# Layer 1's attention in groups of four heads: one PSUM bank per unit, plain transpositions, normalisation at the output, split scores

## The reference, cut to what matters

```python
def swa_mixer(hx, hc, w_in, sink, w_out, with_ctx):        # 16 query heads, 4 key/value heads, head size 64
    qx, kx, vx = qkv_heads(hx, w_in, ...); qc, kc, vc = qkv_heads(hc, w_in, ...)
    qx, kx = axial_rope(qx), axial_rope(kx)
    # per block of 128 queries: latent keys at a distance of at most 128, and all 256 context keys
    #   s = q @ k.T * 64 ** -0.5 + bias;  p = softmax([s, sink])[..., :-1];  o = p @ v
    return unblock(lax.map(block, ...)) @ w_out
```

## Time and profile before

| | us |
|---|---|
| median of 3 runs (lowest, highest) | 3349.37 (3347.96, 3357.53) |
| the profiled execution's own time | 3347.44 |
| its span, first to last instruction | 3345.6 |
| TensorE products busy | 2969.4 (89%) |
| TensorE weight loads busy | 2475.1 (74%) |
| VectorE busy | 2146.4 (64%) |
| ScalarE busy | 1195.6 (36%) |
| mean granted TensorE clock | 0.949 of full speed |

### The profile page before, as it was taken

One profiled execution on the slowest core, in us unless ns is written; L12 is line 12 of the kernel. 1 busy time (PEld: TensorE's weight loads), 2 busy tenths in 40 slices (PEclk: granted clock), 3 DMA queues, 4 the chain that ended last, 5 costly groups with the idle time before them and its releaser, 6 DMA issues.

```text
span 3345.6 us, 45434 instructions
## 1 busy us (share of the span) xinstructions
PE 2969.4 (89%) x16149; PEld 2475.1 (74%) x16149; DVE 2146.4 (64%) x4006; ACT 1195.6 (36%) x2081; POOL 513.3 (15%) x323
## 2 busy tenths in 40 slices
PE   7799987797577999999999999599717899999997
PEld 1488874571476999999999999466616799999997
DVE  0256554399794777777777777534599565666666
ACT  0222220320493333333333333123309444444443
POOL 0000000322102333333333333000510000000000
PEclk9899998898898999999999999889859999999999
DMA  6311111425368787878877877310306656566654
GB/s 260 142 60 63 63 51 51 151 79 199 115 198 287 270 280 271 281 272 281 274 278 276 277 278 247 117 44 32 128 24 176 236 209 211 204 212 213 211 209 144
DMA packets 216326, 616.86 MB, mean 184 GB/s; under 512 B 15496, under 2 KB 97584, under 8 KB 209968
## 3 DMA queue, kind: packets, MB, share of 16 engines
q1 hardware_dynamic: 179388, 481.70, 40.9%
q0 software_dynamic: 36864, 134.23, 11.9%
HBM read 567.54 MB, written 48.33 MB: 184 GB/s over the span
## 4 chain that ended last, share of the span: by engine, by line
PE 75%; DVE 15%; DMA 4%; issue 2%; ACT 2%; DVEq 1%; POOL 1%; SPq 0%; ACTq 0%; POOLq 0%
PE bank L889 27%; PE bank L900 26%; PE bank L693 5%; PE bank L788 2%; DVE arena L1550 2%; DMA arena<-in_wst 2%; PE bank L735 2%; DVE arena L1551 2%; PE bank L700 2%; PE bank L658 2%; PE bank L822 1%; DVE arena L1449 1%; DVE arena L1452 1%; DVE arena L1450 1%; PE bank L975 1%
## 5 line engine op out<-in xcount | busy, mean ns | idle before, releaser
L889 PE MATMUL bank<-h_parts,u_hi 128*128 128x384 f32 (+1 forms) x4096 | 902.5, 311 | 33.0 <-DVE u_lo L1555 33.0
L900 PE MATMUL bank<-v_parts,p_hi 128*128 128x512 f32 x2560 | 794.1, 391 | 0.4 <-DVE p_lo L1571 0.3
L889 PEld LDWEIGHTS bank<-h_parts,u_hi 128*128 128x128 f32 x4096 | 706.7, 191 | 53.7 <-issue 34.2
L889 PE MATMUL bank<-h_parts,u_lo 128*128 128x384 f32 (+1 forms) x2048 | 637.4, 311 | 0.0
L900 PEld LDWEIGHTS bank<-v_parts,p_hi 128*128 128x128 f32 x2560 | 470.8, 188 | 87.6 <-DVE p_lo L1571 1.0
L900 PE MATMUL bank<-v_parts,p_lo 128*128 128x512 f32 x1280 | 500.7, 391 | 0.0
L1567 DVE TENSOR_TENSOR arena<-arena 128x384 f32<-128x384 f32 (+1 forms) x256 | 190.7, 745 | 438.6 <-ACT arena L1190 437.9
L1190 ACT ACTIVATE arena<-bank 128x384 f32<-128x384 f32 (+1 forms) x256 | 111.7, 436 | 974.2 <-PE bank L889 974.2
L889 PEld LDWEIGHTS bank<-h_parts,u_lo 128*128 128x128 f32 x2048 | 391.6, 191 | 0.0
L1555 DVE TENSOR_TENSOR u_lo<-arena,u_hi 128x1024 fp32r<-128x1024 f32 x256 | 312.9, 1223 | 114.8 <-ACT u_hi L1183 86.1
L1569 DVE TENSOR_TENSOR v_parts<-arena,v_parts 128x1024 fp32r<-128x1024 f32 x256 | 313.7, 1225 | 45.9 <-ACT v_parts L1193 37.5
(11 more groups left out here) (216 smaller groups left out, 3629.2 us busy)
## 6 DMA issues: line engine op xcount, KB each, us to landing
arena<-in_u SPq DMA_DIRECT2D x256, 512.0 KB, 4.6
arena<-in_v SPq DMA_DIRECT2D x256, 512.0 KB, 3.6
arena<-in_wst SPq DMA_DIRECT2D x39, 2048.0 KB, 7.6
gate_scratch<-arena SPq DMA_DIRECT2D x20, 2048.0 KB, 8.7
arena<-gate_scratch SPq DMA_DIRECT2D x32, 768.0 KB, 5.0
arena<-in_whd SPq DMA_DIRECT2D x8, 2560.0 KB, 9.1
arena<-gate_scratch SPq DMA_DIRECT2D x32, 512.0 KB, 4.4
x_scratch<-arena SPq DMA_DIRECT2D x10, 512.0 KB, 3.1
```

Source lines behind the costliest of these rows:

```text
L889: last = mm(banks[q][:, 0:ND[p]], w[:, q, col], h[:, k, DS[p]], start=(n3 == 0), stop=(n3 == 3 * KT - 1))
L900: last = mm(banks[2 + 2 * b + half][:, :], x[:, q, b * P:(b + 1) * P], y[:, q, col], start=(first and i == 0), stop=(final and i == 2))
```

## The change

The 32 units are now ordered in groups of four heads that share one key/value head: first the four groups of query block 0, then the four of block 1 (`ATT`).

- **Buffers**: banks 0 to 3 hold the scores of the four units of a group, 4 and 5 the transposed probabilities, 6 and 7 the outputs, one bank for a group's four heads side by side. Probabilities have four buffers instead of two, before and after their transposition.
- **Split scores**: VectorE splits each piece of q and k into a high and a low part, and copies the identity and the mask to fp32r. A score is three split products over 64 rows and one mask product over 128 rows, all in fp32r.
- **Maxima** are reduced one by one, but scaled, compared with the sinks and negated for four units at once. So the first exponential of a group waits for the maxima of all four. The sink's terms are computed once a group.
- **Transpositions** are `nc.tensor.transpose` with the identity; the diagonals are gone.
- **Outputs**: the transposed probabilities (128 columns) are the weights, the values (64 columns) are streamed. The result has the tokens on the rows, and VectorE multiplies four heads at once by the reciprocals (`normalise`) into `o_tok`.
- **Output transpositions**: `o_tok` is transposed by 16 transpositions into `o1`. Eight for block 0 are done during units 29 and 30, eight for block 1 between the first and second output product.
- **Order on TensorE**: four scores ahead; then transpositions of i, scores of i + 4, outputs of i - 1.
- The first score no longer waits for the copy of the values. SP issues `ln_rows` before the two output weight tiles, and `peer_first` after the last output.

```diff
+        ATT = [(kv, b) for b in range(2) for kv in range(4)]
             tile("qkv", 2)
+            ln_rows(1, 0, [1], 8, [2, 3], lambda b: xs[b])
             for i in range(2):
                 tile("wout1", i)
-            sp.wait_ge(at_oc, 32)
-            ln_rows(1, 0, [1], 8, [2, 3], lambda b: xs[b])
+            sp.wait_ge(at_o, 8)
             peer_first(1)
...
             def att_scores(i):
+                kv, b = ATT[i // 4]
+                j, bank = 4 * (kv // 2) + i % 4, banks[i % 4]
+                rows = slice((kv % 2) * SWA_D, (kv % 2 + 1) * SWA_D)
+                cols = slice(b * P, (b + 1) * P)
+                if i >= 4:
+                    pe.wait_ge(at_e, i - 3)
+                for n, (x, y) in enumerate(((q_hi, k_hi), (q_hi, k_lo), (q_lo, k_hi))):
+                    mm(bank[:, :], x[rows, j, cols], y[rows, kv // 2, :], start=(n == 0), stop=False)
                 far = slice(CTX + P, TOK) if b == 0 else slice(CTX, CTX + P)
+                mm(bank[:, far], ident_r, mask_r[:, b, :], start=False, stop=True).then_inc(at_s, 1)
+            def att_transposes(i):
                 pe.wait_ge(at_e, i + 1)
                 if i >= 2:
                     pe.wait_ge(at_tc, i - 1)
                 for c in range(4):
+                    last = nc.tensor.transpose(banks[4 + i % 2][:, c * P:(c + 1) * P], prb[:, i % 4, c * P:(c + 1) * P], ident)
                 last.then_inc(at_t, 1)
+            def att_outputs(i):
+                kv, G, x = ATT[i // 4][0], i // 4, i % 4
                 pe.wait_ge(at_tc, i + 1)
...
                 for c in range(4):
+                    last = mm(banks[6 + G % 2][:, x * SWA_D:(x + 1) * SWA_D], prT[:, i % 4, c * P:(c + 1) * P],
+                              v1[:, c, kv * SWA_D:(kv + 1) * SWA_D], start=(c == 0), stop=(c == 3))
+            for i in range(4):
+                att_scores(i)
+            for i in range(32):
+                att_transposes(i)
+                if i + 4 < 32:
+                    att_scores(i + 4)
+                if i:
+                    att_outputs(i - 1)
+                if i in (29, 30):
+                    out_transposes(0, i - 29, banks[i - 29])
+            att_outputs(31)
...
+            out_product(0, 1)
+            pe.wait_ge(at_oc, 8)
+            for r in range(2):
+                out_transposes(1, r, banks[4 + r])
+            out_product(0, 0)
...
             def exponentials(i):
+                G, x = i // 4, i % 4
+                if x == 0:
+                    act.wait_ge(at_m, G + 1)
...
+                af_(prb[:, i % 4, :], banks[x][:, :], ACT.Exp, scale=SWA_SCALE, bias=st[:, 4 + x:5 + x],
+                    accum_out=st[:, 12 + x:13 + x]).then_inc(at_e, 1)
+                if x == 3:
+                    af_(st[:, 16:20], st[:, 8:12], ACT.Exp).then_inc(at_k, 1)
...
+                link(V.tensor_copy(hi, full))
+                V.tensor_tensor(low, full, hi, ALU.subtract).then_inc(rope, 1)
+            def maxima(G):
...
+                for x in range(4):
+                    dve.wait_ge(at_s, 4 * G + x + 1)
+                    did(V.reduce_max(st[:, x:x + 1], banks[x][:, :], AX.X))
+                st_.wait()
+                link(V.scalar_tensor_tensor(st[:, 0:4], st[:, 0:4], SWA_SCALE, sinks, ALU.mult, ALU.max))
+                did(V.tensor_tensor(st[:, 8:12], sinks, st[:, 0:4], ALU.subtract))
+                st_.wait()
+                V.tensor_scalar(st[:, 4:8], st[:, 0:4], -1.0, None, ALU.mult).then_inc(at_m, 1)
+            def normalise(G):
...
+                dve.wait_ge(at_o, G + 1)
+                out = o_tok[:, b, :].rearrange("p (j x h d) -> p j x h d", j=2, x=4, h=2)[:, kv // 2, :, kv % 2, :]
+                src = banks[6 + G % 2][:, 0:256].rearrange("p (x d) -> p x d", x=4)
+                V.tensor_tensor(out, src, st[:, 12:16].unsqueeze(2).broadcast_to([P, 4, SWA_D]), ALU.mult).then_inc(at_oc, 1)
```

More of the change, by code:

```diff
@@ L273, in build @@
         at_e = sem("swa_exponentials")
[L274 removed]
+        at_k = sem("swa_sink_terms")
         at_t = sem("swa_probs_transposed")
@@ L980, in _ @@
                 pe.wait_ge(at_tc, i + 1)
-                if i >= 2:
-                    pe.wait_ge(at_oc, i - 1)
-                kv = 2 * (j // 4) + half
+                if i == 0:
+                    pe.wait_ge(qk_sb, 11)
+                if x == 0 and G >= 2:
+                    pe.wait_ge(at_oc, G - 1)
                 for c in range(4):
-                    last = mm(banks[4 + i % 2][half * SWA_D:(half + 1) * SWA_D, 0:P], v1[:, c, kv * SWA_D:(kv + 1) * SWA_D],
-                              prT[:, i % 2, c * P:(c + 1) * P], start=(c == 0), stop=(c == 3))
@@ new lines, in _, with out_product @@
+            for i in range(4):
[9 more added lines that the diff above has]
+            att_outputs(31)
+            wslots = [arrived("wout1", half) for half in range(2)]
+            def out_product(b, half):
+                for k in range(KT):
+                    last = mm(banks[2 * b + half][:, :], o1[:, k, b * P:(b + 1) * P], wt(wslots[half])[:, k, :],
+                              start=(k == 0), stop=(k == KT - 1))
+                last.then_inc(y_pe, 1)
@@ L990, in _ @@
+            pe.wait_ge(ot_sb, 2)
+            out_product(0, 1)
[3 more added lines that the diff above has]
+            out_product(0, 0)
+            pe.wait_ge(ot_sb, 4)
+            out_product(1, 0)
+            out_product(1, 1)
             peer(1)
@@ L1640, in _ @@
             dve.wait_ge(swa_c, 16)
+            link(V.tensor_copy(ident_r, ident))
+            did(V.tensor_copy(mask_r, wmask))
             for i in range(10):
[L1642 to L1645, removed]
+                lo = 0 if i < 8 else CTX
                 raw = rawq[:, i % 2, lo:lo + SEQ]
+                full = qsum[:, i % 2, 0:lo + SEQ]
+                dst = qsum[:, i % 2, lo:lo + SEQ]
@@ L1683, in _ @@
-            diagonals(0)
-            for i in range(32):
-                if i < 31:
-                    diagonals(i + 1)
-                if i < 30:
-                    maxima(i + 2)
-                if i:
-                    out_copy(i - 1)
-            out_copy(31)
+                link(V.tensor_tensor(dst, dst, rtmp[:, i % 2, 0:SEQ], ALU.add))
+                hi, low = (q_hi[:, i, :], q_lo[:, i, :]) if i < 8 else (k_hi[:, i - 8, :], k_lo[:, i - 8, :])
+                link(V.tensor_copy(hi, full))
@@ new lines, in out_copy @@
+            def out_copy(n, b, r, bank):
+                dve.wait_ge(ot_pe, n)
+                V.tensor_copy(o1[:, 4 * r:4 * r + 4, b * P:(b + 1) * P], bank.rearrange("p (x t) -> p x t", x=4)).then_inc(ot_sb, 1)
+            maxima(0)
+            for G in range(8):
+                if G < 7:
+                    maxima(G + 1)
+                normalise(G)
+                if G == 6:
+                    for r in range(2):
+                        out_copy(1 + r, 0, r, banks[r][:, :])
+            for r in range(2):
+                out_copy(3 + r, 1, r, banks[4 + r][:, :])
```

128 lines of the change are left out of this document (51 added, 77 removed).

## The result

| | before | after |
|---|---|---|
| median of 15 runs (lowest, highest), us | 3357.53 (3343.11, 3370.12) | 3374.27 (3367.88, 3376.69) |
| ratio of the two, 95% interval | | 1.0051 [1.0036, 1.0066] |
| the profiled execution's own time, us | 3347.44 | 3372.3 |
| its span, us | 3345.6 | 3370.5 |
| its mean granted clock | 0.949 | 0.930 |

What follows compares the result with a forecast made beforehand. TensorE was taken as the bound, resting on its clock. At 1.2 GHz the attention adds 25.3 us and the output product 3.6: 3347.4 + 28.9 = 3376.3 profiled, 3377 for the median, range 3332 to 3388.

Steps and rivals of the forecast that it cites:

- The level: Layer 1's attention: TensorE's clock falls near 2206.9 and stays at 1.2 GHz until the output product; 0.62 with slower loads.
- The rival of a high level: Attention of layer 1: TensorE's clock holds 2.4 GHz or comes back at once, 3314 us; chance 0.14.
- Prices: One unit (one head, 128 queries) on TensorE: 2.48 us at 2.4 GHz against 3.58 before, 4.55 at 1.2 against 6.6.
- a weight load of 128 columns at the low level: Output products at 1.2 GHz: each load costs 0.21 us, so eight cost 1.70 a unit; bounds 0.88 and 1.90.
- The rival in which loads don't get slower: Output products at 1.2 GHz: outputs cost 0.88 a unit and the standstill 1.45, giving 3356 us; chance 0.12.
- The standstill: TensorE waits once a group for the fourth maximum's chain, seven times: 0.65 us each at 1.2 GHz, 1.45 at 2.4.
- The start: From the value product: four scores, the clock falling near 2206.9, then a 2.35 us wait; first transposition at 2210.95.
- The tail: End of the attention loop, counted at 1.2 GHz within 144.2 us from first transposition to last output, ending at 2355.1.
- The output product: Product after the attention: starts at 1.2 GHz and loses 2.6 us, with eight transpositions of 0.9 to 1.0; +3.6 together.
- Costed at nothing: VectorE's extra copies and subtractions of q and k, hidden beside the value product; under 2 us without that cover.

Runs made afterwards that it cites:

- e1_fill_all: Changed kernel plus 108 unread filler products in TensorE's waits, at the start and at each later group: 3319.78 us, ratio 0.99 to the kernel before.
- e3_unit_max: Changed kernel with each unit's maximum scaled, compared and negated by itself, so no joins: three runs 3304.97 to 3306.18 us, three 3367.50 to 3369.08.
- e5_full_rows: Changed kernel with key heads zero-padded so scores use 128 rows, maxima still by group: 3307.77 us, ratio 0.9866 to the kernel before.
- e6_full_unit: Changed kernel with both the per-unit maxima of e3_unit_max and the 128-row key heads of e5_full_rows: 3292.68 us, ratio 0.9821 to the kernel before.
- e4_products: Changed kernel with plain float32 products with the identity in place of the probabilities' transpositions: 3399.68 us, ratio 1.0139 to the kernel before.
- e2_fill_start: Changed kernel with filler products only at the start, the waits between groups left empty: 3364.61 us, ratio 1.0036 to the kernel before.
- e8_unit_rows: e3_unit_max with score products over 128 rows and the mask product over 64, so it computes something else: 3302.95 us, ratio 0.9852 to the kernel before.
- e7_unit_start: e3_unit_max plus two full-row filler products behind each of the first four scores: 3304.13 us, ratio 0.9856 to the kernel before.

## Why the prediction was right, and where its numbers were off

- **The level.** Forecast: 0.50 from 2206.9 to the output product, as likely but not certain. It was so in the profile, from 2211.4 to 2351.3, and the mean clocks of the 15 runs (0.928 to 0.932) leave little room for anything else. e1_fill_all shows that this is the loss: the same work, with its waits filled, is 54.5 us faster at the high level. The rival of a high level was given 3314; with 108 fillers it measured 3319.78.
- **Prices.** Low level, forecast and measured: transpositions 0.88 and 0.85, scores with mask 1.97 and 1.98, outputs 1.70 and 1.71. High level (e1_fill_all): 0.44, 1.16 and 1.15, 0.88 and 0.89. The term that could have made 20 us of difference, a weight load of 128 columns at the low level, came out at 333 ns and 0.21 of time per instruction. The rival in which loads don't get slower is out.
- **The standstill.** Seven joins of 0.65 forecast, 0.76 measured, 0.49 of it idle and 0.27 a load that starts only then. The chain was as written.
- **The start.** The first transposition was forecast 7.75 after the value product and came after 6.78. I had the clock fall at 2206.9, where it fell before, which is in the fourth score; all four ran at 2.4 GHz, and it fell in the wait behind them. 1.0 less.
- **The tail.** From the first transposition to the last output 144.2 was forecast and 142.3 measured. The last units have no scores, the clock came back inside them, and 16 of the outputs took 1.79 instead of 3.4.
- **The output product.** With its transpositions 31.3 was forecast and 28.4 measured. This is the term that was mis-sized: "it starts at the low level and lifts it after some 5 us of which half is lost, 2.6" didn't happen, because the tail had already lifted it. The first 16 products took 6.92, as at the high level.
- The three make 1.0 + 1.9 + 2.9 = 5.8, and 28.9 - 5.8 = 23.1 is what the profiles show in this stretch. The 1.7 us ahead of it were not forecast and are no part of the change.
- **Luck in the total.** The sum was 3376.3 for a profiled run, and 3372.3 was measured; the three terms are 5.8 too dear and the 1.7 us ahead of them hide part of that. The median should then have been 3376.3 + 1.9 = 3378.2 by the prediction's own figures; 3377 is a slip of 1.2 that happens to lie nearer to 3374.27. As a change, 27.6 was forecast (3377 against the 3349.37 of three runs) and 16.7 measured, because 15 runs of the kernel before have a median of 3357.53: the prediction didn't reckon with the second kind of run.
- **Costed at nothing.** VectorE's new copies and subtractions hid as said: from 2190 to 2204, beside the value product, it is busy for 2.69 of 14 us, and from the first product for q to the end of the value product both kernels take 67.6 us. The norm's rows gave and cost nothing that can be seen. The first score starts as the value product ends, where it came 1.25 later before; the sum had that in it.
- **Why it doesn't come back.** The prediction named three reasons at once: standstills, exposed loads, and half-array scores. The runs sort them in part. Removing the joins alone gives a kernel that holds the high level in three of six runs (e3_unit_max). Full rows, which also end the exposed loads, give it back within two units with the joins kept (e5_full_rows). With both repairs it doesn't fall (e6_full_unit). The mode of the transpositions has no part (e4_products). With half rows and joins together it is lost even from a bridged start (e2_fill_start). How much of this is the rows and how much the exposed loads is settled only as far as e8_unit_rows goes, which keeps exposed loads and was short in four runs.

What stays open: why e3_unit_max holds in one run and falls in the next. The Trainium skill ("TensorE: Matmul & The Clock Gate", Part 1: The HAM clock gate) says that the gate's window of activity is free-running and doesn't start anew with the kernel. That would make runs of one kernel differ as they do, and the six runs agree with it, but none of them shows where such a window begins. The two kinds of run of the kernel before (3343 to 3350, 3357 to 3370) may be the same thing, a shorter or longer stay at 0.50 in its first units; I have a profile of the first kind only, so this is argued, not shown.

## What to carry to other kernels

When a change makes TensorE's work in a stretch shorter, price each instruction at both levels of the clock and then ask of the stretch what TensorE does in it without standing still and over all 128 rows; a cheaper unit at 1.2 GHz lost here to a dearer one at 2.4 GHz. Look at the first few us of the stretch and at every place where TensorE waits for a chain of small operations, and take out waits that join units for the sake of a few small instructions on an engine that has time. Where operands fill half of the rows, zeros in the other half cost VectorE a little (3.9 instead of 1.1 us for each of the two pieces of k) and TensorE nothing, and here they were worth 66.5 us (3374.27 to 3307.77), exposed loads included, twice what the change itself could save at 2.4 GHz by the prediction.

## What the runs showed of the hardware

- **The rows that products use go with the level of the clock.** With the same joins, scores over 64 rows stayed at 0.50 (changed kernel, 15 runs of 3368 to 3377) and scores over 128 rows came back to 1.00 (e5_full_rows, 4 runs of 3307 to 3310); there the exposed loads go too. e3_unit_max and e8_unit_rows both have exposed loads and differ in the rows: with 64 three of six runs were long, with 128 none of four. That points to the rows and is too few runs to show it.
- **A low level can last beside a TensorE that is never idle**: 136 us in e3_unit_max, busy 50.00 of 50. At the high level the same loop stays there (e7_unit_start, 1.00). So the same loop can keep either level, and busy time in a profile doesn't tell which; its row of granted clock does.
- **A change of the number of rows exposes a weight load**: the score and mask pair takes 1.15 where scores use 64 rows and the mask 128, and 0.70 + 0.06 = 0.76 where both use 128. That is 0.39 for two changes at the high level, the 0.2 each that the prediction took from the kernel before. In e8_unit_rows, where the mask alone uses 64 rows, the scores behind the transpositions take 0.70, the mask 0.25 and the outputs behind it 1.03 instead of 0.89: the extra time moves to where the rows change.
- **The length of a weight load follows the clock**: 191 ns at 2.4 GHz (e6_full_unit, 224 of them), 333 at 1.2 (168 in the changed kernel). A float32 product with 64 streamed columns is bound by it at both: 0.111 us (e6_full_unit, 0.89 for eight) and 0.214.
- **Work that does nothing can pay**: 108 products, some 13 us of TensorE (1.47 for twelve), made the kernel 54.5 us faster.
